# Dilated sample stage of a decoder step: keys and values of the cached rows loaded by separate requests, and the second tile's keys requested earlier

## The chip, the cores and the metric

The kernel runs on one core of one Trainium2 chip. The metric is the device time of one execution in microseconds (us). A core has five instruction streams: TensorE (PE, the matrix engine; its weight loads are listed apart as PEld), VectorE (DVE), ScalarE (ACT), GpSimd (POOL) and SyncE (SP), which here only sends requests to the 16 DMA engines. Each engine runs its own list in order, and waits on semaphores for the others.

## The reference, cut to what matters

The program is one layer of a hybrid decoder for 512 prompt tokens and 8 sample sequences of 4 new tokens each. Only the sample sequences' dilated attention and their sliding window are touched by the change. In the reference this is

```python
# for g, (window, dil) in enumerate(((128, 1), (512, 4), (2048, 16))):
buf = jnp.concatenate([dil_caches[g][l], jnp.stack([k, v], axis=2)], axis=1)
o, lse = dilated_sample(q, buf[:, :, 0], buf[:, :, 1], n_buf, window, dil)

def dilated_sample(q, k_all, v_all, n_buf, window, dil):
    idx = n_buf + jnp.arange(s_len)[:, None] - dil * jnp.arange(span + 1)[None, :]
    ...
    s = jnp.einsum('bqhe,bqkhe->bhqk', q, kg) * (q.shape[-1] ** -0.5)
    p, lse = masked_softmax(s, valid[None, None])
    o = jnp.einsum('bhqk,bqkhe->bqhe', p.astype(vg.dtype), vg)
```

Every new token attends, in each of three dilated groups (4 heads of 64 channels), to 128 cached rows at distance d, 2d, ... and to itself. A cached row of a dilated group is 512 float32 numbers: first 256 of keys, then 256 of values. Beside it the same rows of the batch attend to a window of 512 cached rows of the sparse mixer (a row is 128 numbers of keys, then 128 of values). Scores need keys alone; values are needed only after the softmax.

## The kernel before, in words

The program is a chain of stages, each one a block: every engine runs its part of the stage, and a barrier of all five engines ends it. The order inside a stage is written out by hand, by semaphores with constant targets; no planner moves anything. The stages around the change are, in time: the prompt's dilated attention; `sample_queries`, which turns the new tokens' queries; `sample_dilated`, the stage that the change is in; `sample_nsa`, the sparse mixer of the sample; then the mixing products and the experts.

`sample_dilated` works on two tiles of four sequences each (`i` = 0 and 1, a hardware loop on PE, ACT and DVE). The cached rows of a tile lie in four buffers of SBUF, one per group, and there is a single copy of each: `kv1` (dilation 4, 4 MiB), `kv2` (dilation 16, 4 MiB), `kvw` (window, 2 MiB) and `kv0` (dilation 1, 1 MiB). In the profile kv0, kv1 and kv2 are all called `sd_kv` (kv1 is `sd_kv_5196` in the order of instructions). A request (one `dma_start`) brings one sequence of one buffer, keys and values together, so a tile takes 16 requests.

For a tile PE does this:

1. Products of the queries with the new tokens' keys (line 1625, 1627).
2. Six steps (`GROUPS`: g1 twice, g2 twice, w, g0). `trans(m)` turns the keys of four sequences, 16 transposes of 128x128 into four PSUM banks (line 1596); DVE copies banks 0 and 2 to SBUF and ACT banks 1 and 3 (line 1682); `score(m)` multiplies (lines 1606 to 1616). The order is trans(0), trans(1), score(0), trans(2), score(1), and so on. Before the first `trans` of a group, PE waits for the semaphore of that group's requests.
3. After the softmax (DVE lines 1712 to 1722, ACT 1689 and 1690), transposes of the probabilities (1638 to 1645), then the products with the values: g1 and g2 (line 1650), g0 (1654), the new tokens (1658, 1661) and the window (1664). Each of the groups raises a semaphore `s_pv[...]` when it is through.
4. DVE scales the result and PE turns it (1730 to 1736).

SP sends kv1 of tile 0 already in `sample_queries`. In `sample_dilated` it sends kv2, kvw and kv0 of tile 0 at once; kv1 of tile 1 waits for `s_pv["g1"]` of tile 0 (the buffer's values have been read), kv2 for `s_pv["g2"]`, kvw and kv0 for `s_pv["w"]`. All of SP's requests are sent in this one order. POOL sends one gather of 2 MiB for the next stage after `s_pv["g1"]` of tile 0 and two more after that of tile 1 (`gather_half`, line 1744).

Of the kernel before, what the change touches and what calls it, by code (L numbers as in the profile page):

```python
# [82 lines left out]
CREDIT = 1  # L83
# [48 lines left out]
class Program:  # L132
# [1240 lines left out]
    def dilated_buffers(self):  # L1373
# [6 lines left out]
        self.s_sd = {kind: self.sem(f"sd_{kind}_loaded") for kind in ("g1", "g2", "w", "g0")}  # L1380

    def load_group1(self, sp, i):

        cache = self.i["cache_dil_w512"][0].rearrange("b t k h d -> b t (k h d)")
        for b in range(4):
            sp.dma_start(self.sd_kv1[:, b], cache[4 * i + b:4 * i + b + 1].rearrange("o (c j) x -> c (o j) x", j=4)
                         ).then_inc(self.s_sd["g1"], 16)

    def sample_queries(self, rows, qrot):
# [6 lines left out]
        with ExitStack() as s:  # L1396
# [20 lines left out]
            with nc.Block() as block:  # L1417
                @block.sync
                def _(sp):
                    self.load_group1(sp, 0)  # L1420
# [76 lines left out]
    def sample_dilated(self, oT):  # L1497
# [6 lines left out]
        with ExitStack() as s:  # L1504
# [49 lines left out]
            with nc.Block() as block:  # L1554
                @block.sync
                def _(sp):
                    for i in range(2):
                        if i > 0:
                            sp.wait_ge(s_pv["g1"], i + CREDIT)
                            self.load_group1(sp, i)  # L1560
                            sp.wait_ge(s_pv["g2"], i + CREDIT)
                        for b in range(4):
                            sp.dma_start(kv2[:, b], caches[2][4 * i + b:4 * i + b + 1].rearrange("o (c j) x -> c (o j) x", j=16)[:, 0:SS, :]
                                         ).then_inc(self.s_sd["g2"], 16)
                        if i > 0:
                            sp.wait_ge(s_pv["w"], i + CREDIT)
                        for b in range(4):
                            sp.dma_start(kvw[:, b], win[4 * i + b:4 * i + b + 1].rearrange("o (c j) x -> c (o j) x", j=4)
                                         ).then_inc(self.s_sd["w"], 16)
                        for b in range(4):  # L1570
                            sp.dma_start(kv0[:, b], caches[0][4 * i + b:4 * i + b + 1].rearrange("o c x -> c (o x)")
                                         ).then_inc(self.s_sd["g0"], 16)
# [12 lines left out]
                def _(pe):  # L1585
                    quarter = [slice(32 * b, 32 * b + 32) for b in range(4)]
                    with pe.Fori(0, 2) as i:
                        def trans(m):
                            kind, ch, n = GROUPS[m]
                            if ch == 0:  # L1590
                                pe.wait_ge(self.s_sd[kind], 64 * i + 64)
# [55 lines left out]
                        for g, kv in enumerate((kv1, kv2)):  # L1647
                            for j in range(SS):
# [3 lines left out]
                            ins.then_inc(s_pv[f"g{g + 1}"], 1)  # L1652
# [1692 lines left out]
```

## Time and profile before

| | us |
|---|---|
| median of 3 runs | 1348.7 |
| the three runs | 1348.7, 1340.48, 1349.47 |
| profiled execution, own time | 1347.1 |
| its span (first to last instruction) | 1345.3 |
| `sample_queries` in it | 525.5 to 545.3 |
| `sample_dilated`, tile 0 | 547.6 to 592.1 |
| `sample_dilated`, tile 1 | 592.5 to 640.6 |
| first instruction of `sample_nsa` | 647.9 |

The times of the stages are read from the timeline of the profiled execution, whose own time is 1.8 us more than its span. In the rows below a time is counted from the first instruction. The "PEclk" of a stretch is the granted clock of TensorE as a share of its full speed of 2.4 GHz: 1.00 is 2.4 GHz and 0.50 is 1.2 GHz.

### The profile page before, as it was taken

The numbers are of one execution on the slowest core, as the hardware profiler recorded it, in microseconds if no ns is written. First come the engines' busy times: TensorE is split into PE (matmuls) and PEld (weight loads), VectorE is DVE, ScalarE is ACT, GpSimd is POOL, SyncE is SP. The second block draws the span as 40 slices with busy tenths as digits, with TensorE's granted clock in tenths as the row PEclk, the third lists the DMA queues.
The fourth block names the chain that finished last, engine by engine and source line by source line (L and its number), as shares of the span: only waits on it lengthen the run. The fifth ranks groups of instructions, "written<-read, shape, count | busy, mean of one in ns | idle before, by whom it ended". The sixth has DMA issues, their size and how long they took to land. (4 is left out here: it accounts for less than half of the span.)

```text
span 1345.3 us, 20451 instructions
## 1 busy us (share of the span) xinstructions
PE 1096.2 (81%) x8164; PEld 819.5 (61%) x8166; DVE 522.1 (39%) x1050; ACT 336.3 (25%) x756; POOL 168.8 (13%) x207
## 2 busy tenths in 40 slices
PE   2999997999899898857698898659995599888750
PEld 2999997999856655645587787548554233333220
DVE  5433332324377675433456466513224311111005
ACT  4000002221346553212345454400011011111002
POOL 0600003200045343000000000000000111110100
PEclk7999998789979998669799999879996699898885
DMA  8122241246489996564253333039505599999944
GB/s 254 41 81 80 80 127 33 83 130 186 148 281 328 328 315 244 219 245 194 108 227 146 149 152 127 0 123 340 203 32 234 205 425 423 421 424 424 422 161 172
DMA packets 75789, 279.68 MB, mean 208 GB/s; under 512 B 16900, under 2 KB 45344, under 8 KB 61856
## 3 DMA queue, kind: packets, MB, share of 16 engines
q1 hardware_dynamic: 66144, 231.09, 47.1%
q0 software_dynamic: 6976, 42.48, 8.2%
q10 hardware_dynamic: 2592, 5.05, 1.0%
q8 instruction: 52, 0.85, 0.3%
q14 instruction: 25, 0.20, 0.0%
HBM read 264.34 MB, written 69.53 MB: 248 GB/s over the span
## 5 line engine op out<-in xcount | busy, mean ns | idle before, releaser
L2908 PE MATMUL ex_up_ps<-ex_w_up,ex_hT 128*64 128x512 f32 x512 | 128.3, 659 | 26.7 <-DMA ex_w_up<-in_expert_w_up 25.7
L123 PE MATMUL proj_acc<-w_in_upper,hT_upper 128*128 128x328 f32 x352 | 111.7, 317 | 13.7 <-DVE w_in_rest L117 7.0
L125 PE MATMUL proj_acc<-w_in_upper,hT_rest 128*128 128x328 f32 x352 | 110.4, 314 | 0.0
L2908 PEld LDWEIGHTS ex_up_ps<-ex_w_up,ex_hT 128*64 128x64 f32 x512 | 42.8, 150 | 100.9 <-issue 92.5
L123 PE MATMUL merge_ps<-hT_upper,merge_w_upper 128*128 128x272 f32 x256 | 79.7, 311 | 5.1 <-DVE merge_w_rest L117 5.1
L124 PE MATMUL proj_acc<-w_in_rest,hT_upper 128*128 128x328 f32 x252 | 79.6, 316 | 0.0
L123 PE MATMUL sn_hp<-sn_xT,cmp_w_upper 128*128 128x256 f32 x256 | 79.3, 310 | 0.0
L124 PE MATMUL merge_ps<-hT_rest,merge_w_upper 128*128 128x272 f32 x256 | 78.6, 307 | 0.0
L125 PE MATMUL merge_ps<-hT_upper,merge_w_rest 128*128 128x272 f32 x256 | 78.4, 306 | 0.0
L124 PE MATMUL sn_hp<-sn_xT,cmp_w_upper 128*128 128x256 f32 x256 | 76.3, 298 | 0.0
L125 PE MATMUL sn_hp<-sn_xT,cmp_w_rest 128*128 128x256 f32 x256 | 76.0, 297 | 0.0
L123 PEld LDWEIGHTS proj_acc<-w_in_upper,hT_upper 128*128 128x128 f32 x352 | 66.7, 190 | 15.2 <-issue 14.6
L3003 DVE TENSOR_TENSOR ex_act<-ex_silu,ex_up_ps 128x256 f32<-128x256 f32 x16 | 6.7, 421 | 156.8 <-ACT ex_silu L2959 156.8
L125 PEld LDWEIGHTS proj_acc<-w_in_upper,hT_rest 128*128 128x128 f32 x352 | 66.6, 189 | 0.0
L2929 PE MATMUL ex_down_ps<-ex_w_down,ex_actT 128*64 128x512 f32 x256 | 58.4, 597 | 1.2 <-ACT ex_actT L2969 1.2
L2440 PE MATMUL mx_ps<-mx_w_out,mx_mixT 128*128 128x512 f32 x128 | 56.2, 594 | 1.0 <-DVE mx_products L2531 1.0
L123 PEld LDWEIGHTS merge_ps<-hT_upper,merge_w_upper 128*128 128x128 f32 x256 | 53.5, 209 | 5.6 <-DVE merge_w_rest L117 5.3
L2428 PE MATMUL mx_ps<-oT,mx_w 128*128 128x272 f32 x192 | 47.0, 410 | 8.4 <-DMA mx_w<-in_w_branch_dil 8.4
L123 PEld LDWEIGHTS sn_hp<-sn_xT,cmp_w_upper 128*128 128x128 f32 x256 | 52.3, 204 | 2.2 <-issue 1.9
L124 PEld LDWEIGHTS merge_ps<-hT_rest,merge_w_upper 128*128 128x128 f32 x256 | 53.3, 208 | 0.0
L125 PEld LDWEIGHTS merge_ps<-hT_upper,merge_w_rest 128*128 128x128 f32 x256 | 53.2, 208 | 0.0
L125 PEld LDWEIGHTS sn_hp<-sn_xT,cmp_w_rest 128*128 128x128 f32 x256 | 52.7, 206 | 0.0
(465 smaller groups left out, 2121.3 us busy)
## 6 DMA issues: line engine op xcount, KB each, us to landing
ex_w_up<-in_expert_w_up SPq DMA_DIRECT2D x32, 2048.0 KB, 28.5
ex_w_down<-in_expert_w_down SPq DMA_DIRECT2D x32, 1024.0 KB, 30.6
out_dil_sample<-in_cache_dil_w SPq DMA_DIRECT2D x8, 4088.0 KB, 28.2
sd_kv<-in_cache_dil_w SPq DMA_DIRECT2D x16, 1024.0 KB, 10.4
w_in_chunk<-in_w_in SPq DMA_DIRECT2D x11, 1312.0 KB, 6.0
merge_w<-in_w_in SPq DMA_DIRECT2D x16, 512.0 KB, 5.1
out_dil_sample<-in_cache_dil_w SPq DMA_DIRECT2D x8, 1016.0 KB, 20.2
merge_gates_scratch<-qT_dil ACTq DMA_DIRECT2D x16, 272.0 KB, 4.4
```

Of the source, the lines that this page charges most:

```text
L123: pe.matmul(out, a[0], b[0], start=first, stop=False)
L124: pe.matmul(out, a[0], b[1], start=False, stop=False)
L125: return pe.matmul(out, a[1], b[0], start=False, stop=last)
L2428: ins = pe.matmul(ps[:, 4 * (m % 2) + 2 * p + half, 0:HT], w[:, c0 + k, m * P:(m + 1) * P], oT[:, c0 + k, half * HT:(half + 1) * HT], star ...
L2440: ins = pe.matmul(ps[:, n % 3, :], mixT[:, k, t * P:(t + 1) * P], wo[:, k, half * 512:(half + 1) * 512], start=k == 0, stop=k == KD - 1)
L2908: ins = pe.matmul(up_ps[r, q, :], hT[:, q, c, r], wu[slot][:, u, c, :], start=c == 0, stop=c == KD - 1)
L2929: ins = pe.matmul(dn_ps[r, half, :], aT[:, q, c, r], wd[slot][:, u, c, half * 512:(half + 1) * 512], start=c == 0, stop=c == 1)
L3003: dve.tensor_tensor(ac[:, q, :], sl[:, q, :], up_ps[:, q, FF:2 * FF], ALU.mult).then_inc(s_ac, 1)
```

## The change

Every request is split in two: one for the key half of each row and one for the value half. A tile now takes 32 requests, of 512 KiB (kv1, kv2), 256 KiB (kvw) and 128 KiB (kv0). A piece that is contiguous in memory was 8 KiB (kv1 and kv2: four neighbouring rows), 4 KiB (kvw) and 2 KiB (kv0) per partition; it is now 1 KiB, 512 bytes and 1 KiB. The number of bytes is the same. There are two semaphores per buffer, `s_sd[0]` for keys and `s_sd[1]` for values; PE waits for the first before `trans` and for the second before the products with the values.

SP sends the keys of all groups of tile 0 first, then their values. Then it waits on the count of transposed banks, `s_tp` (four per step): after step 1 it sends tile 1's keys of kv1, after step 3 those of kv2, after step 4 those of kvw, after step 5 those of kv0. The values of tile 1 wait for `s_pv`, as the whole buffers did.

```diff
@@ -1377,14 +1377,15 @@
         self.sn_raw_at = at - 4 * STRIDE // 2 * 4 * KVD
         self.sn_raw = self.nc.alloc_sbuf_tensor_at("sn_raw", [P, RAW, STRIDE // 2, 4 * KVD], F32, offset=self.sn_raw_at)
         self.s_raw = [self.sem(f"sn_raw_loaded{j}") for j in range(RAW)]
-        self.s_sd = {kind: self.sem(f"sd_{kind}_loaded") for kind in ("g1", "g2", "w", "g0")}
-
-    def load_group1(self, sp, i):
-
+        self.s_sd = [{kind: self.sem(f"sd_{part}_{kind}_loaded") for kind in ("g1", "g2", "w", "g0")} for part in "kv"]
+
+    def load_group1(self, sp, i, part):
+
+        cols = slice(part * DD, (part + 1) * DD)
         cache = self.i["cache_dil_w512"][0].rearrange("b t k h d -> b t (k h d)")
         for b in range(4):
-            sp.dma_start(self.sd_kv1[:, b], cache[4 * i + b:4 * i + b + 1].rearrange("o (c j) x -> c (o j) x", j=4)
-                         ).then_inc(self.s_sd["g1"], 16)
+            sp.dma_start(self.sd_kv1[:, b, :, cols], cache[4 * i + b:4 * i + b + 1, :, cols].rearrange("o (c j) x -> c (o j) x", j=4)
+                         ).then_inc(self.s_sd[part]["g1"], 16)
 
     def sample_queries(self, rows, qrot):
 
@@ -1417,7 +1418,8 @@
             with nc.Block() as block:
                 @block.sync
                 def _(sp):
-                    self.load_group1(sp, 0)
+                    self.load_group1(sp, 0, 0)
+                    self.load_group1(sp, 0, 1)
 
                 @block.tensor
                 def _(pe):
@@ -1554,22 +1556,43 @@
             with nc.Block() as block:
                 @block.sync
                 def _(sp):
-                    for i in range(2):
-                        if i > 0:
-                            sp.wait_ge(s_pv["g1"], i + CREDIT)
-                            self.load_group1(sp, i)
-                            sp.wait_ge(s_pv["g2"], i + CREDIT)
+                    def load_group2(i, part):
+                        cols = slice(part * DD, (part + 1) * DD)
                         for b in range(4):
-                            sp.dma_start(kv2[:, b], caches[2][4 * i + b:4 * i + b + 1].rearrange("o (c j) x -> c (o j) x", j=16)[:, 0:SS, :]
-                                         ).then_inc(self.s_sd["g2"], 16)
-                        if i > 0:
-                            sp.wait_ge(s_pv["w"], i + CREDIT)
+                            sp.dma_start(kv2[:, b, :, cols], caches[2][4 * i + b:4 * i + b + 1, :, cols]
+                                         .rearrange("o (c j) x -> c (o j) x", j=16)[:, 0:SS, :]).then_inc(self.s_sd[part]["g2"], 16)
+
+                    def load_win(i, part):
+                        cols = slice(part * KVD, (part + 1) * KVD)
                         for b in range(4):
-                            sp.dma_start(kvw[:, b], win[4 * i + b:4 * i + b + 1].rearrange("o (c j) x -> c (o j) x", j=4)
-                                         ).then_inc(self.s_sd["w"], 16)
+                            sp.dma_start(kvw[:, b, :, cols], win[4 * i + b:4 * i + b + 1, :, cols]
+                                         .rearrange("o (c j) x -> c (o j) x", j=4)).then_inc(self.s_sd[part]["w"], 16)
+
+                    def load_group0(i, part):
+                        cols = slice(part * DD, (part + 1) * DD)
                         for b in range(4):
-                            sp.dma_start(kv0[:, b], caches[0][4 * i + b:4 * i + b + 1].rearrange("o c x -> c (o x)")
-                                         ).then_inc(self.s_sd["g0"], 16)
+                            sp.dma_start(kv0[:, b, cols], caches[0][4 * i + b:4 * i + b + 1, :, cols].rearrange("o c x -> c (o x)")
+                                         ).then_inc(self.s_sd[part]["g0"], 16)
+
+                    for part in range(2):
+                        load_group2(0, part)
+                        load_win(0, part)
+                        load_group0(0, part)
+                    sp.wait_ge(s_tp, 8 + CREDIT)
+                    self.load_group1(sp, 1, 0)
+                    sp.wait_ge(s_tp, 16 + CREDIT)
+                    load_group2(1, 0)
+                    sp.wait_ge(s_tp, 20 + CREDIT)
+                    load_win(1, 0)
+                    sp.wait_ge(s_tp, 24 + CREDIT)
+                    load_group0(1, 0)
+                    sp.wait_ge(s_pv["g1"], 1 + CREDIT)
+                    self.load_group1(sp, 1, 1)
+                    sp.wait_ge(s_pv["g2"], 1 + CREDIT)
+                    load_group2(1, 1)
+                    sp.wait_ge(s_pv["w"], 1 + CREDIT)
+                    load_win(1, 1)
+                    load_group0(1, 1)
 
                 @block.gpsimd
                 def _(pool):
@@ -1588,7 +1611,7 @@
                         def trans(m):
                             kind, ch, n = GROUPS[m]
                             if ch == 0:
-                                pe.wait_ge(self.s_sd[kind], 64 * i + 64)
+                                pe.wait_ge(self.s_sd[0][kind], 64 * i + 64)
                             for b in range(4):
                                 if m > 0:
                                     pe.wait_ge(s_ev[b % 2], 12 * i + 2 * m + b // 2 - 1 + CREDIT)
@@ -1645,11 +1668,13 @@
                         pe.transpose(tq[0:TS, 3 * P:4 * P], ew[:, 512:544], self.ident[:, :]).then_inc(s_tp2, 1)
                         pe.wait_ge(s_pt, 5 * i + 5 + CREDIT)
                         for g, kv in enumerate((kv1, kv2)):
+                            pe.wait_ge(self.s_sd[1][f"g{g + 1}"], 64 * i + 64)
                             for j in range(SS):
                                 for b, r0 in enumerate(quarter):
                                     ins = pe.matmul(Op[r0, 0:DD], pTz[:, g, j, r0], kv[:, b, j, DD:2 * DD],
                                                     start=g == 0 and j == 0, stop=False)
                             ins.then_inc(s_pv[f"g{g + 1}"], 1)
+                        pe.wait_ge(self.s_sd[1]["g0"], 64 * i + 64)
                         for b, r0 in enumerate(quarter):
                             ins = pe.matmul(Op[r0, 0:DD], pT0[:, r0], kv0[:, b, DD:2 * DD], start=False, stop=False)
                         ins.then_inc(s_pv["g0"], 1)
@@ -1659,6 +1684,7 @@
                                           start=False, stop=g == 2)
                         for b, r0 in enumerate(quarter):
                             pe.matmul(Op[r0, DD:DD + KVD], pTn[:, 3, r0], self.vnew[:, KVD:2 * KVD], start=True, stop=False)
+                        pe.wait_ge(self.s_sd[1]["w"], 64 * i + 64)
                         for a in range(4):
                             for b, r0 in enumerate(quarter):
                                 ins = pe.matmul(Op[r0, DD:DD + KVD], pTw[:, a * P + 32 * b:a * P + 32 * b + 32],
```

Three places show it in the order of instructions. In brackets stand the semaphores that an instruction waits for, by the hardware semaphore's first name in the program; names are reused, and so say nothing of their use here. A row with "xN" is N alike.

SP before, in `sample_dilated`, from its start to its end (`proj_accumulated1`, `proj_copied_by_act` and `proj_copied_by_dve` are `s_pv` of g1, g2 and w):

```order
L1563 DMA sd_kv<-in_cache_dil_w 128x2048 x4
L1568 DMA sd_kvw<-in_cache_nsa_win 128x1024 x4
L1571 DMA sd_kv<-in_cache_dil_w 128x512 x4
L1386 DMA sd_kv_5196<-in_cache_dil_w 128x2048 [waits proj_accumulated1]
L1386 DMA sd_kv_5196<-in_cache_dil_w 128x2048 x3
L1563 DMA sd_kv<-in_cache_dil_w 128x2048 [waits proj_copied_by_act]
L1563 DMA sd_kv<-in_cache_dil_w 128x2048 x3
L1568 DMA sd_kvw<-in_cache_nsa_win 128x1024 [waits proj_copied_by_dve]
L1568 DMA sd_kvw<-in_cache_nsa_win 128x1024 x3
L1571 DMA sd_kv<-in_cache_dil_w 128x512 x4
```

SP now, from the values of tile 0 to the first values of tile 1 (the keys of tile 0 stand ahead of it, in the same three kinds; `cmp_bias_copied` is `s_tp`, `merge_w_loaded1` is `s_pv` of g1):

```order
L1562 DMA sd_kv<-in_cache_dil_w 128x4x256 x4
L1568 DMA sd_kvw<-in_cache_nsa_win 128x4x128 x4
L1574 DMA sd_kv<-in_cache_dil_w 128x256 x4
L1387 DMA sd_kv_5196<-in_cache_dil_w 128x4x256 [waits cmp_bias_copied]
L1387 DMA sd_kv_5196<-in_cache_dil_w 128x4x256 x3
L1562 DMA sd_kv<-in_cache_dil_w 128x4x256 [waits cmp_bias_copied]
L1562 DMA sd_kv<-in_cache_dil_w 128x4x256 x3
L1568 DMA sd_kvw<-in_cache_nsa_win 128x4x128 [waits cmp_bias_copied]
L1568 DMA sd_kvw<-in_cache_nsa_win 128x4x128 x3
L1574 DMA sd_kv<-in_cache_dil_w 128x256 [waits cmp_bias_copied]
L1574 DMA sd_kv<-in_cache_dil_w 128x256 x3
L1387 DMA sd_kv_5196<-in_cache_dil_w 128x4x256 [waits merge_w_loaded1]
```

The four sets of tile 1's keys moved ahead of the wait for `s_pv` of g1 and stand behind all requests of tile 0.

PE now, at the products with the values (before, the rows of lines 1674, 1679 and 1690 were lines 1650, 1654 and 1664, and of these only the first had a wait, a single one):

```order
L1669 ISA
L1674 MATMUL sd_O<-sd_kv_5196,sd_pTz 32x256 [waits x_loaded4,merge_w_loaded0]
L1674 MATMUL sd_O<-sd_kv_5196,sd_pTz 32x256 x15
L1674 MATMUL sd_O<-sd_kv,sd_pTz 32x256 [waits identity_loaded]
L1674 MATMUL sd_O<-sd_kv,sd_pTz 32x256 x15
L1679 MATMUL sd_O<-sd_kv,sd_pT 32x256 [waits eps_and_zeros_ready]
L1679 MATMUL sd_O<-sd_kv,sd_pT 32x256 x3
L1683 MATMUL sd_O<-sample_place,sd_pTn 32x256 x12
L1686 MATMUL sd_O<-sample_place,sd_pTn 32x128 x4
L1690 MATMUL sd_O<-sd_kvw,sd_pTw 32x128 [waits gain_loaded]
```

Four waits are added per tile, one before each group's first product with its values; nothing else on PE moved, and DVE, ACT and POOL have the same instructions in the same order.

## Rows read from the trace of the kernel before

**Rows 1.** Who waited for whom, 592 to 625 us: us in total, times, longest

```profile
PE sd_tp L1596 <- DMA sd_kv<-in_cache_dil_w: 5.2, 2, 2.8
```

**Rows 2.** Timeline of tile 1 (start, us, engine, line, op), idle before in brackets

```profile
598.42 0.61 PE L1627 MATMUL sd_O<-sample_place,sd_qTw 128*128 128x32 f32 x2
601.79 6.60 PE L1596 MATMUL sd_tp<-ident,sd_kv 128*128 128x128 f32 x32 [2.75 <-DMA sd_kv<-in_cache_dil_w]
608.32 1.08 PE L1616 MATMUL sd_Sd<-sd_kT,sd_qTz 128*32 128x128 f32 x32
611.85 1.96 PE L1596 MATMUL sd_tp<-ident,sd_kv 128*128 128x128 f32 x16 [2.45 <-DMA sd_kv<-in_cache_dil_w]
...
620.56 1.09 PE L1596 MATMUL sd_tp<-ident,sd_kv 128*128 128x128 f32 x8
```

**Rows 3.** The same steps in tile 0, timeline

```profile
554.30 6.45 PE L1596 MATMUL sd_tp<-ident,sd_kv 128*128 128x128 f32 x32
...
560.67 1.08 PE L1616 MATMUL sd_Sd<-sd_kT,sd_qTz 128*32 128x128 f32 x32
561.69 1.97 PE L1596 MATMUL sd_tp<-ident,sd_kv 128*128 128x128 f32 x16
```

**Rows 4.** SP's requests, timeline 515 to 660 us: start, time over all of them

```profile
525.54 2.60 SPq L1386 DMA_DIRECT2D sd_kv<-in_cache_dil_w  x4
547.59 1.97 SPq L1563 DMA_DIRECT2D sd_kv<-in_cache_dil_w  x4
...
584.48 1.96 SPq L1386 DMA_DIRECT2D sd_kv<-in_cache_dil_w  x4
586.48 2.01 SPq L1563 DMA_DIRECT2D sd_kv<-in_cache_dil_w  x4
589.29 8.04 SPq L1568 DMA_DIRECT2D sd_kvw<-in_cache_nsa_win  x4
```

**Rows 5.** Stretches: length, busy PE, PEld, DVE, ACT, POOL (x), PEclk, DMA share, GB/s

```profile
610.00:617.00 7.00, 5.15 (x77) 4.63 (x81) 2.76 (x4) 2.02 (x4) 0.00 (x0) 1.00 1.01 402
```

**Rows 6.** A stretch of 1312-byte pieces, columns as in Rows 5

```profile
187.00:190.00 3.00, 3.00 (x22) 3.00 (x21) 0.00 (x0) 0.00 (x0) 0.00 (x0) 1.00 1.04 385
```

**Rows 7.** Two stretches of 512-byte pieces, columns as in Rows 5

```profile
190.80:192.00 1.20, 1.20 (x10) 1.20 (x10) 0.88 (x1) 0.00 (x0) 0.00 (x0) 1.00 1.21 292
330.00:334.00 4.00, 4.00 (x34) 4.00 (x33) 1.24 (x2) 0.80 (x2) 0.00 (x0) 1.00 0.57 128
```

**Rows 8.** Timeline of the stage's end and of the next one's start

```profile
634.17 0.95 POOL L1744 DMA_INDIRECT sn_raw<-in_cache_nsa_paged,page_rows  x1 [47.60 <-PE sd_O L1650]
...
640.43 0.19 DVE L1736 COPY oT<-sd_tq 128x32 f32 x1 [0.83 <-PE sd_tq L1669]
647.87 3.70 ACT L2096 CAST cmp_w_upper<-cmp_w 128x2048 fp32r<-128x2048 f32 x2 [16.73 <-PEq L1554]
```

**Rows 9.** Transfers of POOL's queue from 645 to 648 us: packets, MB, share

```profile
q0 software_dynamic: 46, 0.49, 38.5%
```

**Rows 10.** Timeline, first and last products with the values, tile 0 and tile 1

```profile
581.17 4.96 PE L1650 MATMUL sd_O<-sd_kv,sd_pTz 128*32 128x256 f32 x64 [0.66 <-ACT sd_pTn L1695]
...
588.14 1.08 PE L1664 MATMUL sd_O<-sd_kvw,sd_pTw 128*32 128x128 f32 x32
...
631.19 3.86 PE L1650 MATMUL sd_O<-sd_kv,sd_pTz 128*32 128x256 f32 x64 [0.66 <-ACT sd_pTn L1695]
...
637.06 1.08 PE L1664 MATMUL sd_O<-sd_kvw,sd_pTw 128*32 128x128 f32 x32
```

**Rows 11.** PEclk by stretches of 3 us, columns as in Rows 5

```profile
557.00:560.00 3.00, 3.00 (x16) 3.00 (x15) 1.39 (x2) 0.89 (x2) 0.00 (x0) 0.51 0.98 411
560.00:563.00 3.00, 3.00 (x51) 2.63 (x50) 1.31 (x2) 1.05 (x3) 0.00 (x0) 1.00 1.05 416
...
605.00:608.00 3.00, 3.00 (x17) 3.00 (x16) 1.04 (x3) 1.17 (x2) 0.00 (x0) 0.54 1.02 423
608.00:611.00 3.00, 1.40 (x36) 0.96 (x34) 0.68 (x1) 0.59 (x1) 0.00 (x0) 1.00 1.00 412
```

## The prediction

> **What bounds the kernel now.** I read the list of waits first, restricted to the stage, then the timeline of both tiles on PE, then SP's requests and the transfer rates. The waits show where DMA is in PE's way: only in tile 1, twice, 5.2 us together [rows 1]. (The other rows of a wait on DMA are PE's weight loads at the same moments; they are not added.) The timeline puts the two waits: PE has finished the new tokens' keys at 598.42 + 0.61 = 599.03 and starts trans(0) 2.75 us later, because the keys of kv1 come with its values, and both could only be requested at 584.48, when the last product with kv1 of tile 0 was through; then score(0) ends at 609.40 and trans(2) starts 2.45 us later, for kv2 [rows 2]. The later groups are in time: trans(5) starts at 620.56 with no DMA before it. In tile 0 the same steps run without a break: trans(0) at 554.30, score(0) to 561.75, trans(2) at 561.69 [rows 3]. While PE waits in tile 1 the queues are full, 402 GB/s at a share of 1.01 [rows 5], so the loads are late because they are asked for late, and because values travel ahead of keys that are needed sooner.
>
> The stage ends in a second chain. PE and DVE are through at 640.62, yet the next stage starts at 647.87. In between POOL's queue still moves the two gathers it sent at 634.17, when g1 of tile 1 was through [rows 8]; their last 0.49 MB go between 645 and 648 us [rows 9]. I read this as the stage's barrier waiting for the gathers, though the list only names the barrier. Both chains hang on PE reaching the products with the values of tile 1, so time saved before that reaches the end, and time lost behind it has up to 7 us of cover.
>
> **The change, part by part.**
>
> *Tile 1's keys early.* Tile 0 moves kv2 4.19 MB, kvw 2.10, kv0 1.05 = 7.34 MB from 548.5 (the first request is sent at 547.59 [rows 4], and about 1 us goes by until data move). Tile 1's keys add 2.10 + 2.10 + 1.05 + 0.52 = 5.77 MB. What rate do short pieces give? The nearest row for 1 KiB is the projection's weights, in pieces of 328 numbers, 1312 bytes: 385 GB/s at a full share [rows 6]. For 512 bytes it is the merge weights, 128 numbers a piece: 292 GB/s while the share is full, and at worst 128 GB/s at a share of 0.57, that is 225 at full share [rows 7]. I take 385 for 1 KiB and 292 for 512 bytes, since both rows are taken with the queue full, as here. Tile 0's 5.24 MB of 1 KiB pieces take 13.6 us and its 2.10 MB of 512 bytes 7.2: until 569. Tile 1's kv1 keys (permitted at 561, two steps into tile 0) then land by 575, kv2 by 580, kvw by 584, kv0 by 585. PE would want them at 599.0, at 599.0 + 7.6 = 606.6 (7.6 is from trans(0)'s start to score(0)'s end in rows 2), and the last at 620.56 - 5.2 = 615.4. So both waits go: **-5.2 us**. If all pieces moved at 292, the 13.1 MB would be in by 548.5 + 44.9 = 593.4, still before 599. The saving is bounded by the two waits; no other DMA wait is there to be taken.
>
> The Trainium skill, "DMA: Bandwidth & Descriptors", puts the smallest transfer for line rate at 512 bytes, and in its section "Bandwidth" says to batch requests to 1 MiB or more for 75% of peak or better, which speaks against this change. By its fit, 2.0 us and the bytes at 436 GB/s, a 512 KiB request alone gets 164 GB/s and a 256 KiB one about 101. The trace does not agree for requests that queue behind one another: it has 402 GB/s with 512 and 256 KiB requests among them in the queue [rows 5], and 292, not the full rate, at 512 bytes [rows 7]. By the trace the sum stays -5.2; by the Trainium skill's fit the keys would be late again (slow rival).
>
> *SP.* A request costs SP about 0.49 us (1.97 over 4 [rows 4]). Eight in place of four ahead of the stage: 5 us, or at most the 4.19 MB at 292, 14 us, if SP is held up by a full queue; both end by 541, before that stage ends at 545.3. In the stage, SP's 24 first requests may hold it until about 569, as its third set held it 8.04 us before [rows 4]; the four sets of keys go out behind them, some 20 us ahead of need. **0.** If this cover went, the keys would be late by what is missing.
>
> *Values.* Tile 0's are in by 569, wanted from 581.17 [rows 10]. Tile 1's are sent from 584.5, as before; 7.34 MB with one gather of 2.1 MB at the rates above (26 us) end at about 611, wanted at 631.19 - 5.2 = 626. At 225 GB/s they would end at 626.5: just at the edge. **0.**
>
> *PE's added waits.* Four per tile. No row shows this wait alone. From below it costs nothing, as the matmuls ahead of it are still in the array; from above, the 0.66 us of PE before line 1650 [rows 10], which is a real wait for ACT, so too much. I take 0.1 us each; four in tile 0 and the first in tile 1 lie on the chain: **+0.5 us** (0 to 3.3). The last three are behind POOL's release and covered by the 7 us.
>
> *The clock.* PE's granted clock is 0.50 when either tile starts turning keys, and full after some 6 us of it: by 560 in tile 0, by 608 in tile 1 [rows 11], also with the 2.75 us idle before it. I expect the rise inside trans(1) again. What it can give or take: the products with the values took 588.14 + 1.08 - 581.17 = 8.0 us in tile 0, where the clock rose late, and 6.9 in tile 1 [rows 10]; 16 transposes at half clock are half of 6.45 against 1.97 at full [rows 3], 1.3 us more. With two such places and the next stage's start, +-3 us; **0** in the sum.
>
> *Sum.* -5.2 + 0.5 = -4.7 us on the profiled execution: 1347.1 to 1342.4, the span 1345.3 to 1340.6. The profiled execution lies 1.6 below the median of the three runs, 1348.7, and these spread over 9 us without any change; -4.7 on the median gives 1344.0. I forecast **1343**, between the two.
>
> **The rivals.**
>
> *Forecast: the two waits go, 2 to 8 us less*, 1340.7 to 1346.7 on the median. Chance 0.72.
>
> *The waits go and the clock takes it back.* If the clock rises one step later in tile 1's transposes (+1.3), the values of tile 1 run at tile 0's pace (+1.1) and the next stage's start loses as much (+1.5), the gain is under 1 us: 1348. For it: the two tiles differ in just this. Against: there are fewer idle gaps than before. Chance 0.14.
>
> *Slower: short pieces starve tile 1.* The place is still trans(0) and trans(2) of tile 1, now for the whole queue ahead of them: 13.1 MB have to pass by 615.4, 66.9 us after 548.5. That needs 196 GB/s on average (11.5 MB by 606.6 needs 198). Below it the gain shrinks, and it turns at about 182: then the last keys are in at 620.6, where they are now wanted. At 150 GB/s the last keys come at 548.5 + 87.4 = 635.9, 15.3 us behind the present 620.6: 1364. For it: packets are up to eight times as many, and one row has 225. Against: 292 and 385 with the queue full. By the fit of the Trainium skill above, requests of this size would run under 182 GB/s, which is this rival. Chance 0.06.
>
> *The stage's end does not follow*, because something other than the values of tile 1 holds the 7 us gap: if it is a fixed cost of changing stages the gain stays; if it were bound to a time of its own, as a transfer started at 585, it is lost: 1348.7. The only transfers in the gap start at 634 [rows 8], against it. Chance 0.04.
>
> *More than the waits:* the clock helps in all three places, 9 to 10 us less, 1339. Chance 0.04.
>
> **How the numbers follow.** The forecast's own bounds are 1340.7 to 1346.7; the runs before lie up to 8 us below and 1 above their median, so a median of as many can lie 4 us to either side. That gives 1335 to 1350, which also holds the clock rival, the end that does not follow and the bigger gain; left out are the slow rival and the tails. One per cent, 13.5 us, is about what a measurement of this kernel tells from no change. A gain over that would be nearly three times the DMA waits there are: 0.04, all for the spread of runs. Slower by that needs the starving at 153 GB/s or less: 0.04. Within: 0.92.
>
> **What would show it.** The two waits for `sd_kv` gone from PE's list, trans(2) of tile 1 about 7.5 us behind its trans(0) instead of 10.1; tile 1's kv1 keys landed before 580 and the queues idle between about 585 and the values' requests; the gathers sent at about 629.5 and `sample_nsa` starting about 643. Packets of SP's queue up by some 22,500, rates in the stage 290 to 390 GB/s. Wrong would be: waits for DMA ahead of trans in either tile, or ahead of line 1674; rates under 200; or a gap behind DVE's last copy that has grown by what was saved.

## The result, and the profile after

| | before | changed |
|---|---|---|
| median, first 20 runs of each | 1348.84 us | 1339.45 us |
| lowest to highest of them | 1340.48 to 1353.26 | 1333.57 to 1345.03 |
| median, a second set (29 and 12 runs) | 1345.65 | 1338.65 |
| span of the profile | 1345.3 | 1341.9 |

The ratio of changed to before is 0.9937 with a 95% interval of 0.992 to 0.9955 in the first set and 0.9952 (0.9927 to 0.9976) in the second. As differences of the means this is -8.4 +- 1.2 us and -7.1 +- 1.2 us (standard errors). The forecast was 1343 from 1348.7, -5.7 us with 4.7 of it from the sum. The kernel is faster by more than noise, and by somewhat more than forecast.

The span of the two profiles differs by 3.4 us only, and that number says nothing of the change. In the profile after, the stage before the changed one starts at 529.54 where it started at 525.54 [rows 4]; nothing ahead of that point was changed. So each stage has to be read from its own start. SP's requests in the changed stage, in the timeline of the changed kernel (start, time over all of them, number):

```profile
529.54 8.40 SPq L1387 DMA_DIRECT2D sd_kv<-in_cache_dil_w  x8
552.86 2.05 SPq L1562 DMA_DIRECT2D sd_kv<-in_cache_dil_w  x4
554.95 4.90 SPq L1568 DMA_DIRECT2D sd_kvw<-in_cache_nsa_win  x4
559.89 2.60 SPq L1574 DMA_DIRECT2D sd_kv<-in_cache_dil_w  x4
...
572.54 2.60 SPq L1574 DMA_DIRECT2D sd_kv<-in_cache_dil_w  x4
575.18 3.43 SPq L1387 DMA_DIRECT2D sd_kv<-in_cache_dil_w  x4
578.65 6.40 SPq L1562 DMA_DIRECT2D sd_kv<-in_cache_dil_w  x4
585.10 5.81 SPq L1568 DMA_DIRECT2D sd_kvw<-in_cache_nsa_win  x4
590.95 3.81 SPq L1574 DMA_DIRECT2D sd_kv<-in_cache_dil_w  x4
594.81 7.39 SPq L1387 DMA_DIRECT2D sd_kv<-in_cache_dil_w  x4
```

These answer to [rows 4]. The first four requests take SP 0.51 us each, as before; the later ones take 0.6 to 1.9 us, which I read as SP being held up by full queues. Tile 1's first keys, permitted after two steps of tile 0, go out at 575.18, 22.3 us into the stage, because SP's list puts them behind all of tile 0's values; the last set of keys is sent from 590.95 on. That is still far ahead of PE, in the timeline of tile 1:

```profile
603.11 0.61 PE L1650 MATMUL sd_O<-sample_place,sd_qTw 128*128 128x32 f32 x2
603.54 6.26 PE L1619 MATMUL sd_tp<-ident,sd_kv 128*128 128x128 f32 x32
609.74 1.08 PE L1639 MATMUL sd_Sd<-sd_kT,sd_qTz 128*32 128x128 f32 x32
610.75 1.97 PE L1619 MATMUL sd_tp<-ident,sd_kv 128*128 128x128 f32 x16
```

Against [rows 2] both brackets with a wait for DMA are gone: trans(0) follows the line before it at once, and trans(2) starts 7.2 us behind trans(0) instead of 10.1. The list of waits of the stage has no row with DMA left. The transfer rates of the changed kernel (length, busy engines, PEclk, DMA share, GB/s) answer to [rows 5 to 7]. The first two stretches have pieces of 1 KiB (in the first, 2.11 MB in 2128 packets), the last has pieces of 512 bytes (0.86 MB in 1692 packets):

```profile
584.00:590.00 6.00, 5.34 (x59) 2.76 (x61) 1.29 (x4) 1.16 (x2) 0.00 (x0) 0.64 1.09 352
605.00:611.00 6.00, 6.00 (x61) 5.63 (x60) 2.44 (x4) 2.35 (x4) 0.00 (x0) 0.68 1.09 348
572.00:575.00 3.00, 3.00 (x64) 2.63 (x56) 1.38 (x2) 1.26 (x3) 0.00 (x0) 1.00 1.19 287
```

Short pieces cost bandwidth: 350 and 287 GB/s here, against 421 with pieces of 8 KiB from 592 to 611 us before. It stayed hidden. The row of SP's queue in the page of the profile shows the number of packets, which was 66144 before:

```profile
q1 hardware_dynamic: 89184, 231.09, 48.8%
```

The end of the stage, timeline, against [rows 8]:

```profile
634.22 0.95 POOL L1770 DMA_INDIRECT sn_raw<-in_cache_nsa_paged,page_rows  x1 [42.95 <-PE sd_O L1674]
...
640.90 0.19 DVE L1762 COPY oT<-sd_tq 128x32 f32 x1 [1.24 <-PE sd_tq L1695]
647.80 3.70 ACT L2122 CAST cmp_w_upper<-cmp_w 128x2048 fp32r<-128x2048 f32 x2 [17.62 <-PEq L1556]
```

From SP's first request in the stage to the start of the next one it is 647.80 - 552.86 = 94.9 us, where it was 647.87 - 547.59 = 100.3: 5.3 us less. The gap at the end, from DVE's last copy to the next stage, is 6.7 us, where it was 7.3. Behind it the sparse stage (up to the first load of the mixing stage, 893.1 and 895.5) took 245.3 us against 247.6, with the same instructions.

### The profile page after: what moved, and what is told of

Read it like the earlier page. It is cut to its first block and busy times, and to the rows that moved or that the text cites. A ratio compares the mean times of both kernels' runs of the same rounds, so it can differ in the third digit from the quotient of the medians.

```text
span 1341.9 us, 20487 instructions
## 1 busy us (share of the span) xinstructions
PE 1098.9 (82%) x8166; PEld 819.7 (61%) x8166; DVE 521.9 (39%) x1050; ACT 336.4 (25%) x756; POOL 169.7 (13%) x207
## 5 line engine op out<-in xcount | busy, mean ns | idle before, releaser
L123 PE MATMUL sn_hp<-sn_xT,cmp_w_upper 128*128 128x256 f32 x256 | 78.1, 305 | 0.0
L124 PE MATMUL sn_hp<-sn_xT,cmp_w_upper 128*128 128x256 f32 x256 | 74.8, 292 | 0.0
L123 PEld LDWEIGHTS sn_hp<-sn_xT,cmp_w_upper 128*128 128x128 f32 x256 | 50.9, 199 | 2.2 <-issue 1.9
L124 PEld LDWEIGHTS sn_hp<-sn_xT,cmp_w_upper 128*128 128x128 f32 x256 | 51.3, 200 | 0.0
```

The source lines that it names most:

```text
L123: pe.matmul(out, a[0], b[0], start=first, stop=False)
L124: pe.matmul(out, a[0], b[1], start=False, stop=False)
```

## The experiments

Each was run with a profile. The table gives for each the length of the dilated stage, the wait for DMA before PE's transposes in tile 1, the gap between DVE's last copy and the next stage, the length of the sparse stage (all from the profile's timeline), and the difference of the mean of its timed runs from that of the kernel before on the same chip, with its standard error. Where the last column is empty, the profiled run is the only one. "Changed, 2nd profile", "halves, not early" and the two kernels with late gathers are compared with the same 29 runs of the kernel before, so their differences are not independent; so are "first gather later" and "all gathers moved", with the same 23.

| kernel | stage | DMA wait | gap | sparse stage | timed runs |
|---|---|---|---|---|---|
| before | 100.3 | 5.2 | 7.3 | 247.6 | |
| before, 2nd profile | 101.8 | 5.4 | 7.0 | 249.4 | |
| before, 3rd profile | 100.6 | 5.3 | 7.1 | 245.6 | |
| before, 4th profile | 101.2 | 5.4 | 6.9 | 249.3 | |
| changed | 94.9 | 0 | 6.7 | 245.3 | -8.4 +- 1.2 |
| changed, 2nd profile | 94.8 | 0 | 7.1 | 244.9 | -7.1 +- 1.2 |
| changed, 3rd profile | 95.6 | 0 | 6.7 | 245.3 | |
| changed, 4th profile | 95.1 | 0 | 6.9 | 248.6 | |
| halves, not early | 95.7 | 0 | 6.9 | 248.7 | -7.5 +- 1.3 |
| halves, old order | 106.1 | 7.3 | 6.8 | 245.0 | |
| first gather later | 97.2 | 0.9 | 6.9 | 249.8 | +0.2 +- 1.7 |
| change + one gather late | 89.4 | 0 | 1.8 | 250.1 | -6.0 +- 1.2 |
| change + both gathers late | 87.9 | 0 | 0.3 | 244.9 | -13.7 +- 1.3 |
| before, all gathers moved | 88.8 | 0.8 | 0.3 | 247.9 | -7.5 +- 1.5 |

**The changed kernel again.** No edit.

> The changed kernel once more, for the spread of its stages. The dilated sample stage takes 95.0 us from SP's first request to the start of the next stage in the profile after, against 100.3 before: 5.3 us, while the 20 timed runs of each differ by 8.4 us. Theory (the rest is scatter of other stages, which hold the same instructions): this profile has the stage at 95 +- 1 us again, and the sparse stage behind it anywhere from 242 to 250 us (245.2 after, 247.7 before). Rival (the change also shortens the sparse stage, by its place against the clock): the sparse stage is again at 245 us or less and the time is 0.6% below before.

The stage was 94.8 us and the sparse stage 244.9; the timed runs gave 0.9952. Both the theory's ranges and the rival's short sparse stage came true (the time was 0.5% below before, and not 0.6%), so this run does not tell them apart. Whether the change has a share in the short sparse stage is what the last four profiles take up.

**Halves, but not early.**

```diff
-                    sp.wait_ge(s_tp, 8 + CREDIT)
+                    sp.wait_ge(s_pv["g1"], 1 + CREDIT)
                     self.load_group1(sp, 1, 0)
-                    sp.wait_ge(s_tp, 16 + CREDIT)
+                    sp.wait_ge(s_pv["g2"], 1 + CREDIT)
                     load_group2(1, 0)
-                    sp.wait_ge(s_tp, 20 + CREDIT)
+                    sp.wait_ge(s_pv["w"], 1 + CREDIT)
                     load_win(1, 0)
-                    sp.wait_ge(s_tp, 24 + CREDIT)
                     load_group0(1, 0)
-                    sp.wait_ge(s_pv["g1"], 1 + CREDIT)
                     self.load_group1(sp, 1, 1)
-                    sp.wait_ge(s_pv["g2"], 1 + CREDIT)
                     load_group2(1, 1)
...
```

> Requests in halves as in the change, but tile 1's keys are not asked for early: kv1's keys wait for the last product with kv1's values of tile 0, kv2's for that with kv2, the others for the window's, and all values come behind all keys. Theory A (the halves alone are enough): keys of kv1 are 2.1 MB, asked for at 5 us into the products with the values, and land some 8 us later, about 6 us before PE wants them; kv2's 14 us later, also in time. No wait for DMA before trans, stage at 95 to 96 us, time like the change's (0.993 to 0.996 of before). Theory B (asking early is what removes the waits): PE waits 1 to 3 us at trans(0) and trans(2) of tile 1, stage at 98 to 100 us, time 0.998 to 1.0 of before.

Theory A holds: no wait for DMA, stage 95.7 us, ratio 0.9948 (0.9924 to 0.9971), the same as the change's. The timeline of tile 1:

```profile
592.48 0.61 PE L1646 MATMUL sd_O<-sample_place,sd_qTw 128*128 128x32 f32 x2
593.05 6.29 PE L1615 MATMUL sd_tp<-ident,sd_kv 128*128 128x128 f32 x32
599.27 1.08 PE L1635 MATMUL sd_Sd<-sd_kT,sd_qTz 128*32 128x128 f32 x32
600.28 1.97 PE L1615 MATMUL sd_tp<-ident,sd_kv 128*128 128x128 f32 x16
```

kv1's keys were asked for at 578.54, after the last product with kv1's values as in the kernel before, and were there within 14.5 us, before PE wanted them. Asking for tile 1's keys as soon as tile 0's are turned, the second half of the change, adds nothing that can be measured.

**Halves in the order of the kernel before.**

On the changed kernel, in place of the waits on `s_tp`:

```diff
-                    sp.wait_ge(s_tp, 8 + CREDIT)
+                    sp.wait_ge(s_pv["g1"], 1 + CREDIT)
                     self.load_group1(sp, 1, 0)
...
                     self.load_group1(sp, 1, 1)
                     sp.wait_ge(s_pv["g2"], 1 + CREDIT)
+                    load_group2(1, 0)
                     load_group2(1, 1)
...
```

> Requests in halves, but tile 1's in the order of the kernel before: kv1 keys, kv1 values, then kv2 keys, kv2 values, and so on, each after the products that free it. Theory (what the halves give is that values no longer stand ahead of keys): kv1's keys arrive in time, trans(0) does not wait; kv2's keys stand behind kv1's values, at about 350 GB/s and with the gather they land at 608 to 610 on before's scale, so trans(2) waits 1 to 3 us and the stage is at 97 to 98 us. Rival (size of the requests matters, not their order): no wait, 95 us.

The order is what matters, but I had the size wrong: the stage was 106.1 us, 5 us longer than with whole rows, in the one run that was taken (its whole time was 1351.1 us, against a mean of 1345.6 before on the same chip). In the timeline of tile 1:

```profile
606.87 1.08 PE L1635 MATMUL sd_Sd<-sd_kT,sd_qTz 128*32 128x128 f32 x32
612.56 3.41 PE L1615 MATMUL sd_tp<-ident,sd_kv 128*128 128x128 f32 x16 [4.61 <-DMA sd_kv<-in_cache_dil_w]
615.90 1.25 PE L1635 MATMUL sd_Sd<-sd_kT,sd_qTz 128*32 128x128 f32 x32
617.08 1.96 PE L1615 MATMUL sd_tp<-ident,sd_kv 128*128 128x128 f32 x16
618.97 1.08 PE L1635 MATMUL sd_Sd<-sd_kT,sd_qTz 128*32 128x128 f32 x32
622.24 2.88 PE L1615 MATMUL sd_tp<-ident,sd_kvw 128*128 128x128 f32 x16 [2.19 <-DMA sd_kvw<-in_cache_nsa_win]
```

trans(0) is in time, as expected; trans(2) waits 4.6 us, trans(4) another 2.2 and trans(5) 0.5, 7.3 us together where whole rows had 5.3. The other 3 us are PE's pace behind the waits, where PEclk is 0.50 again: 16 transposes take 3.41 and 2.88 us instead of 1.97, and two steps of score 1.25 and 1.78 instead of 1.08. With the halves alone only the first group's keys gain priority; all later keys stand behind values again, and come at the lower rate. The price of short pieces, hidden in the change, stands here in the open.

**The first gather later, whole rows.** On the kernel before:

```diff
-                    pool.wait_ge(s_pv["g1"], 1 + CREDIT)
+                    pool.wait_ge(s_tp, 48 + CREDIT)
                     pool.nop(nofuse=True)
                     self.gather_half(pool, 0)
```

> The kernel before, whole rows in one request, nothing asked for early. Only POOL's first gather of 2.1 MB, which in the kernel before starts together with tile 1's loads, is held until all keys of tile 1 are turned. Theory (the loads of tile 1 are late because they share the queues with the gather): kv1's 4.19 MB need 10 us from 584.5 instead of 16, so they are there at about 597, 2 us before PE wants them, and kv2 at about 606.5, when PE wants it; both waits go or leave under 0.5 us, the stage is at 95 to 96 us and the time like the change's, 0.994 to 0.996 of before. Rival (whole rows are simply too much to bring behind the last use): the waits stay at 2 us or more.

The mechanism is there: trans(0) does not wait, and for trans(2) 0.94 us are left. In the timeline:

```profile
600.36 6.25 PE L1596 MATMUL sd_tp<-ident,sd_kv 128*128 128x128 f32 x32
608.56 1.96 PE L1596 MATMUL sd_tp<-ident,sd_kv 128*128 128x128 f32 x16 [0.94 <-DMA sd_kv<-in_cache_dil_w]
```

So without 2.1 MB of a gather that runs beside tile 1's loads, and is needed 60 us later, 4.3 of the 5.2 us are gone. The stage was 97.2 us, 3.8 us below the mean of before: the products with the values of tile 1 took 8.8 us here, 0.7 more than the mean of before. But the 12 timed runs show no gain: ratio 0.9995 (0.9965 to 1.0025). That misses the expected 0.994 to 0.996. A stage shorter by 3.8 us and a difference of +0.2 +- 1.7 us don't fit well; the profile's own run had the sparse stage at 249.8 us. What the other runs had there isn't known.

**One gather late.** On the changed kernel: of the two gathers at the end of the stage, the second goes to the head of the next.

```diff
-                    for g in range(1, RAW):
-                        self.gather_half(pool, g)
+                    self.gather_half(pool, 1)
...
                 def _(pool):
+                    self.gather_half(pool, 2)
                     for g in range(RAW, 2 * BS):
```

> The change, and the second of the two gathers that POOL sends at the end of the stage is sent as the first thing of the next stage instead. Theory (the barrier at the stage's end waits until POOL's gathers have landed): with 2.1 MB less in flight the gap between DVE's last copy and the next stage's first instruction shrinks from 7.0 us to about 2 to 3; the next stage needs that third buffer only later, so the time falls by another 4 to 5 us, 0.990 of before. Rival (the gap is a fixed cost of changing to this stage, such as fetching its code): gap still 7 us, and the time stays at the change's or is worse by what the next stage waits for the late gather.

The theory on the gap holds, the expectation of the time doesn't: gap 1.8 us and stage 89.4, but ratio 0.995 (0.9925 to 0.9974), the same as the change's, and not 0.990. In the profile the sparse stage was 250.1 us, 5 us longer than in the profile after. The gap in the timeline:

```profile
637.70 0.19 DVE L1761 COPY oT<-sd_tq 128x32 f32 x1 [1.25 <-PE sd_tq L1694]
639.73 3.71 ACT L2122 CAST cmp_w_upper<-cmp_w 128x2048 fp32r<-128x2048 f32 x2 [12.71 <-PEq L1556]
```

**Both gathers late.** The same with both, `for g in range(1, RAW)` moved as a whole, and its wait dropped, since the stage's end orders it.

> The change, with both gathers of the stage's end sent as the first thing of the next stage. Theory (the barrier waits for gathers to land): the gap falls to about 2 us, as at the start of this stage (545.3 to 547.6 before), so the next stage starts 5 us earlier; but it wants the second buffer about 9 us after its start and the gather needs 7 to 8 us, so that it may wait 0 to 2 us; the time is 3 to 5 us below the change's. Rival (fixed cost): the gap stays 7 us and the next stage waits for the second buffer, so the time is up to 2 us above the change's.

The gap is 0.3 us. The timeline at the end of the stage:

```profile
639.43 0.19 DVE L1758 COPY oT<-sd_tq 128x32 f32 x1 [1.25 <-PE sd_tq L1691]
639.92 3.70 ACT L2120 CAST cmp_w_upper<-cmp_w 128x2048 fp32r<-128x2048 f32 x2 [11.16 <-PEq L1556]
639.98 0.11 DVE L2279 MEMSET sn_xT<- 128x64 f32 x1 [0.36 <-PEq L1556]
640.58 0.95 POOL L1766 DMA_INDIRECT sn_raw<-in_cache_nsa_paged,page_rows  x1 [50.67 <-SPq L1883]
```

So the 7 us at the end of the stage were the gathers in flight. PE and DVE have no wait for DMA in the first 30 us of the sparse stage, so the later buffers are still in time, and this version is the best run here: 1331.77 us against 1345.65 before and 1338.65 of the changed kernel on the same chip, ratio to before 0.9898 (0.9864 to 0.9931, 6 runs).

**All gathers moved, whole rows.** The kernel before with the first gather after tile 1's last transposes and the two others at the head of the sparse stage.

> The kernel before with whole rows, its first gather held until tile 1's keys are turned, and the two last gathers sent as the first thing of the next stage. Theory (both of the stage's losses come from where the gathers stand): stage at 88 us as with both gathers late on the changed kernel, time 0.989 to 0.991 of before without any split request. The three gathers then follow within some 20 us, the first asked for at about 74 us into the stage, lands by 84. Rival: kv1 or kv2 still late by 2 to 5 us, stage 90 to 93 us, 0.993.

The stage is at 88.8 us with 0.8 us of DMA wait left, as expected; the time is at 0.9944 (0.9915 to 0.9973), better than before, but not the 0.990 expected. As with the first gather later, 4 to 5 us of what the stage gives aren't in the timed runs. In the profiles this stage, with whole rows, is within 0.9 us of the changed kernel's with both gathers late: where the gathers are moved, splitting the requests has little left to give. The timed runs can't rank the two: their intervals, 0.9864 to 0.9931 and 0.9915 to 0.9973, overlap.

**Four more profiles, for the sparse stage.** In the first ten profiles its length went with the time at which PE's granted clock rises to 1.00 and stays there, counted from the stage's start. Two more profiles each of the kernel before and of the changed one were to tell whether a kernel has its own length. A fifth, the kernel before again, had been taken earlier:

> The kernel before once more, for the spread of its stages. So far the sparse stage behind the changed one has one of two lengths in the profiles: 245 us (after, after again, both gathers late) or 248 to 250 us (before, halves not early, one gather late); in the short ones PE's clock is 1.00 from 60 to 70 us into the stage, in the long ones 0.66 to 0.83. Theory P (the kernel sets the length, since each stage's first busy stretch starts the same way against the clock): before has 247.6 us again, and the dilated stage 100.3 +- 0.5. Theory R (chance): it may as well be 245.

It gave 249.4 us, and the dilated stage 101.8, outside the +- 0.5 expected. The four:

> In ten profiles the length of the sparse stage follows from when PE's clock rises for good after the stage's start: rises at 11.8, 11.8, 11.9 and 12.3 us went with 244.9, 244.9, 245.0 and 245.3 us, rises at 11.1, 11.5, 12.1, 12.9, 13.4 and 13.7 with 247.6, 247.9, 248.7, 249.4, 249.8 and 250.1. The kernel before had 11.1 and 12.9, the changed one 12.3 and 11.8. Theory P (the stage before sets how the start lies against the clock, so each kernel has its own length): before has 247 to 250 us again. Theory R (chance): before shows 245 us in some of these looks. DMA waits in tile 1 5.2 to 5.4 us, dilated stage 100 to 102 us, in either case.

> Theory P: rise at 11.8 to 12.3 us after the start of the sparse stage and its length 244.9 to 245.4 us, for the third time. Theory R: a rise somewhere between 11 and 14 us, and a length up to 250. The dilated stage 94.8 to 95.2 us without a wait for DMA, in either case.

> As for the third look at the kernel before. Theory P: sparse stage 247 to 250 us. Theory R: anything from 245 to 250.

> As for the third look at the changed kernel. Theory P: sparse stage 244.9 to 245.4 us. Theory R: anything from 245 to 250.

They gave 245.6, 245.3, 249.3 and 248.6 us, with rises at 12.6, 12.3, 12.9 and 12.1. Theory P falls: each kernel shows both lengths. Profiles with the same rise have the same length: 245.3 twice at 12.3 (changed, first and third profile), 249.3 and 249.4 at 12.9 (both of before), 248.6 and 248.7 at 12.1 (the fourth of the changed kernel, and the halves that are not early). But that the rise decides the length isn't shown: a rise at 11.9 went with 245.0 and one at 12.1 with 248.6, and nothing here explains why. What tells the two kinds apart in all fourteen profiles is the clock in the seventh 10 us of the stage. Its mean is 1.00 in the six short ones and 0.66 to 0.83 in the eight long ones. Here it is from 707.8 on in the short profile after, and from 706.2 on in the long fourth one of the changed kernel (columns as above):

```profile
707.80:717.80 10.00, 6.88 (x52) 5.52 (x49) 5.22 (x18) 7.35 (x12) 0.94 (x1) 1.00 0.52 201
```

```profile
706.20:716.20 10.00, 6.88 (x35) 6.05 (x34) 5.71 (x19) 5.37 (x8) 0.94 (x1) 0.66 0.55 212
```

In the same 10 us PE is as busy, but at a PEclk of 0.66 it gets through 35 matmuls instead of 52.

## Why the prediction came out as it did, step by step

*The two waits, -5.2.* Right, and in four profiles of each kernel: 5.2 to 5.4 us before, none after. The explanation was half right. I wrote that the loads are late because they are asked for late and because values travel ahead of keys. The second is what the change mends: halves with the keys first do it without asking early, and halves without the order make it worse by 5 us. And as an explanation of the waits I left out a third cause that stood in the timeline: POOL's first gather, sent at 585.39, shares the DMA engines with tile 1's loads, and holding it back takes 4.3 us of the waits away with whole rows.

*The rates.* 385 and 292 GB/s were taken from [rows 6, 7]; measured are 350 for 1 KiB and 287 in a stretch with 512 bytes. The first was 10% high; its row had longer pieces, of 1312 bytes. SP sent tile 1's first keys 22.3 us into the stage, where I had tile 0's loads end at 569 - 547.6 = 21.4. The slow rival needed less than 196 GB/s and was far off. The Trainium skill, "DMA: Bandwidth & Descriptors", section "Anatomy of one DMA — SWDGE (gpsimd) path", gives its fit for a transfer that GpSimd sends, and by that fit 164 GB/s is an estimate for 512 KiB alone. The traces don't agree for SP's requests that queue behind one another: 350 GB/s.

*SP and the values, 0.* Right in the result. SP's eight requests ahead of the stage took 8.4 us instead of the 5 expected, hidden: from SP's first request there to the changed stage it is 22.0 to 23.7 us in the eight profiles with halves as in the six with whole rows. Two details came out otherwise. I had put 7.34 MB for tile 1's values, which is what tile 0 loads inside the stage; the value halves of a tile are 5.77 MB, and with the gather they need 21 us by my rates and not 26. And I expected the queues to be idle between tile 1's keys and its values. SP was still sending keys at 594.8, 42 us into the stage, and only then sent the values, 5 us later in the stage than I had them. They ran until 618 and were wanted at 630.24, a cover of 12 us where the prediction had 15 (611 against 626).

*PE's added waits, +0.5.* They cost nothing that shows: the idle before line 1674 is 0.66 us as in [rows 10], and the products with the values take 7.9 and 8.0 us in the profile after, within the 6.9 to 8.5 of the four profiles of before. This term was too large by the whole 0.5.

*The stage's end.* Right, and shown: the gap follows the gathers, 7 us with two in flight, 1.8 with one, 0.3 with none. My reading that it would stay and move along was right for this change.

*The clock, 0 +- 3, and what was mis-sized.* The profile of before that the sum was made against had 6.9 us for the values of tile 1 [rows 10]; its three other profiles had 8.4 or 8.5, and the changed kernel 7.9 to 8.0 in all four. The first and last products in the second profile of before, then in the profile after:

```profile
625.36 5.41 PE L1650 MATMUL sd_O<-sd_kv,sd_pTz 128*32 128x256 f32 x64 [0.66 <-ACT sd_pTn L1695]
632.77 1.08 PE L1664 MATMUL sd_O<-sd_kvw,sd_pTw 128*32 128x128 f32 x32
```

```profile
630.24 4.86 PE L1674 MATMUL sd_O<-sd_kv,sd_pTz 128*32 128x256 f32 x64 [0.66 <-ACT sd_pTn L1721]
637.11 1.08 PE L1690 MATMUL sd_O<-sd_kvw,sd_pTw 128*32 128x128 f32 x32
```

So single profiles mislead here, and the means of four are the better measure: the stage has 101.0 us before and 95.1 changed, a gain of 5.9 us and not 4.7. By terms of the sum, as means of four:

| | before | changed | gain | in the sum |
|---|---|---|---|---|
| waits for DMA | 5.3 | 0 | 5.3 | 5.2 |
| PE's added waits | | nothing seen | 0 | -0.5 |
| the first 32 transposes, both tiles | 12.6 | 12.3 | 0.3 | 0 |
| products with the values, both tiles | 16.0 | 15.8 | 0.1 | 0 |
| gap at the end | 7.1 | 6.9 | 0.2 | 0 |

The gains are rounded from unrounded means. The added waits were the largest error inside the stage; the rest is 0.4 us at the two places of the clock, 0.2 us of the gap and 0.1 us of the waits. Behind the stage, the sparse stage is 248.0 us on average before and 246.0 changed, 1.9 +- 1.2 less. Together that is 7.8 us, about what the timed runs have (-8.4 and -7.1). For this second part the sum had nothing but the clock's +- 3. That it belongs to the change isn't shown: both kernels show both lengths, and four profiles of each can't tell 3 of 4 short from 1 of 4 short. So the mechanism of the forecast was right, and its centre was too small by what the sum had at +0.5 and at 0.

The chance of 0.92 for a result within 1% was right, and 1339.45 lies in the range of 1335 to 1350. The median is 3.6 us below the forecast of 1343 and within half a microsecond of the 1339 of "more than the waits", which had 0.04. That rival had the clock help in all three places by 9 to 10 us. The profiles don't show that: in the stage the clock gives about half a microsecond, and for the sparse stage it is open. So the number agrees with the rival's by luck, as far as the runs tell. Part of it is the draw of runs as well, since the second set gave 7.1 us.

Of the signs that I named, these came true: no wait for `sd_kv` on PE, trans(2) 7.2 us behind trans(0), 23040 packets more, rates of 287 to 352 GB/s, and a gap that did not grow. The idle queues between keys and values did not.

*Open.* For three kernels (first gather later, one gather late, all gathers moved) the stage in the profile gained 4 to 6 us more than the timed runs, while for both gathers late the two agree (13.1 and 13.7). The sparse stage's two lengths could do that, were these kernels unlucky in most runs, and so could the scatter of some 10 us in when the stage ahead starts; only one profile of each was taken.

## What to carry to other kernels

When a buffer with two uses is loaded in one request, first ask which half is late and what else is in the queues at that moment. Here ordering keys before values paid for splitting the rows; splitting alone cost 5 us in its one run, and asking early brought nothing more. Look at what is in flight at a stage's end: two prefetches that nobody needed yet held the barrier for 7 us, more than the DMA waits that the change was about. And compare stages from their own starts, with more than one profile, when the effect is under 1%: the stage ahead of the changed one started between 519.5 and 529.5 us in fourteen profiles, with nothing changed before it.

## What the runs showed of the hardware that was not expected

- A stage's barrier waited for the indirect gathers that POOL had sent, though no instruction of the stage waits for them: gap 6.7 to 7.3 us with two gathers of 2.1 MB, the first of them sent 6.3 to 6.7 us before the last copy, 1.8 us with one, 0.3 us with none. In the same gap SP's requests were long done, so the runs don't tell whether SP's own would do the same.
- At a full share of the DMA engines, 8 KiB pieces moved at 421 GB/s (592 to 611 us before), pieces of mostly 4 KiB at 402 [rows 5], 1 KiB pieces at 350, 512-byte pieces at 287 to 292.
- The same instructions of the sparse stage took 244.9 to 250.1 us, and the time in the stage at which PE's clock rose for good went with it, but in no order that the runs explain: 244.9 to 245.6 for rises at 11.8, 11.8, 11.9, 12.3, 12.3 and 12.6 us, 247.6 to 250.1 for 11.1, 11.5, 12.1, 12.1, 12.9, 12.9, 13.4 and 13.7. Two profiles with the same rise, to 0.1 us, agree within 0.2 us in all four such pairs.
